# Key normalisation factors by a product with ones of the squared keys, instead of row sums turned into diagonal matrices

## The reference, cut to what matters

```
k = concatenate([k_nope, broadcast(k_pe)])      # 128 + 64 values a head
q = rms_norm_2(q, q_gain)
k = rms_norm_2(k, k_gain)                       # x * rsqrt(mean(x*x) + 1e-6) * gain
q = concatenate([q[..., :128], rope(q[..., 128:], pos)])
k = concatenate([k[..., :128], rope(k[..., 128:], pos)])
o = mla_attend(q, k, v, pos)                    # softmax of q k^T / sqrt(192), times v
x = x + (o * silu(gate)) @ w_out
```

## Time and profile before

| | before |
|---|---|
| three timed runs | 3512.02, 3507.12, 3512.03 us; median 3512.02 |
| the profiled execution | 3514.65 us |
| its span, first to last instruction | 3512.9 us |
| TensorE busy, share of the span | 96% |
| VectorE busy | 49% |
| ScalarE busy | 34% |
| mean granted clock of TensorE | 0.976 |

### The profile page before, as it was taken

One profiled execution on the slowest core, in us unless ns is written; L12 is line 12 of the kernel. 1 busy time (PEld: TensorE's weight loads), 2 busy tenths in 40 slices (PEclk: granted clock), 3 DMA queues, 4 the chain that ended last, 5 costly groups with the idle time before them and its releaser, 6 DMA issues. The chain is left out here.

```text
span 3512.9 us, 51809 instructions
## 1 busy us (share of the span) xinstructions
PE 3358.3 (96%) x21928; PEld 2646.9 (75%) x21928; DVE 1715.1 (49%) x2838; ACT 1190.1 (34%) x1864; POOL 112.0 (3%) x90
## 2 busy tenths in 40 slices
PE   4999999989999989989999999999999999999999
PEld 2877777767777778857786666787888778887687
DVE  3325555544555545364436556434454455544632
ACT  4113333423333322242224444332333333333421
POOL 1000000001001101100000000010000000000000
PEclk7999999999999989999999999999999999999999
DMA  5522333232212134232342112353322232322442
GB/s 172 139 68 78 93 91 96 81 88 72 63 51 80 52 107 146 83 120 75 95 122 69 36 46 77 96 157 96 96 84 85 75 91 87 91 87 75 150 136 87
DMA packets 492315, 324.38 MB, mean 92 GB/s; under 512 B 27050, under 2 KB 448397, under 8 KB 491446
## 3 DMA queue, kind: packets, MB, share of 16 engines
q1 hardware_dynamic: 492086, 321.08, 31.2%
HBM read 276.18 MB, written 44.85 MB: 91 GB/s over the span
## 5 line engine op out<-in xcount | busy, mean ns | idle before, releaser
L532 PE MATMUL PS<-XH,WHT 128*128 128x512 f32 x2256 | 929.4, 412 | 48.4 <-DVE WLT L520 33.4
L520 DVE TENSOR_TENSOR WLT<-AR,WHT 128x1024 fp32r<-128x1024 f32 (+1 forms) x430 | 520.7, 1214 | 858.0 <-ACT WHT L514 857.4
L534 PE MATMUL PS<-XH,WLT 128*128 128x512 f32 x2256 | 890.1, 395 | 0.0
L514 ACT ACTIVATE WHT<-AR 128x1024 fp32r<-128x1024 f32 (+1 forms) x430 | 446.6, 1041 | 751.8 <-PE PS L534 595.2
L533 PE MATMUL PS<-XL,WHT 128*128 128x512 f32 (+1 forms) x1744 | 684.6, 393 | 0.0
L532 PEld LDWEIGHTS PS<-XH,WHT 128*128 128x128 f32 x2256 | 426.1, 189 | 158.2 <-DVE WLT L520 34.3
L534 PEld LDWEIGHTS PS<-XH,WLT 128*128 128x128 f32 x2256 | 425.8, 189 | 99.7
L533 PE MATMUL PS<-ARR,WHT 128*128 128x512 f32 x1024 | 403.6, 394 | 0.0
L533 PEld LDWEIGHTS PS<-XL,WHT 128*128 128x128 f32 (+1 forms) x1744 | 328.8, 189 | 73.5 <-issue 4.8
L533 PEld LDWEIGHTS PS<-ARR,WHT 128*128 128x128 f32 x1024 | 193.9, 189 | 50.9 <-issue 8.6
L532 PE MATMUL PS<-XL,WHT 128*128 128x512 f32 x512 | 203.6, 398 | 0.0
(11 more groups left out here) (433 smaller groups left out, 5079.8 us busy)
## 6 DMA issues: line engine op xcount, KB each, us to landing
AR<-b_w_in SPq DMA_DIRECT2D x128, 512.0 KB, 4.0
AR<-w_in SPq DMA_DIRECT2D x122, 512.0 KB, 3.7
AR<-a_w_in SPq DMA_DIRECT2D x48, 512.0 KB, 4.3
AR<-w_out SPq DMA_DIRECT2D x32, 512.0 KB, 4.4
AR<-a_w_out SPq DMA_DIRECT2D x32, 512.0 KB, 4.0
AR<-b_w_out SPq DMA_DIRECT2D x32, 512.0 KB, 4.0
proj_scratch<-AR SPq DMA_DIRECT2D x33, 256.0 KB, 2.3
AR<-a_w_kv_up SPq DMA_DIRECT2D x32, 256.0 KB, 3.7
```

The lines of the kernel that those rows point to most:

```text
L514: self.nc.scalar.activation(self.shaped(self.high, n), self.shaped(self.raw, n), ACT.Copy).then_inc(self.s_high, 1)
L520: self.nc.vector.tensor_tensor(self.shaped(self.low, n), self.shaped(self.raw, n), f32(self.shaped(self.high, n)), ALU.subtract).then_inc( ...
L532: mm(out, wh, xh[k0 + c], start=(start and c == 0), stop=False)
L534: last = mm(out, wl, xh[k0 + c], start=False, stop=(stop and c == nk - 1))
```

## The change

- Key sums, their reciprocals and the diagonals are gone. `key_factors` multiplies ones by the squared keys themselves, so each of the 128 partitions of `FB[e]` holds every token's sum of squares. It stands at its old place, behind `value(i, 1)`; for pair 0 it takes the place of the key sums, behind tile 14.
- The mean is taken at full width, 128x512 a head, from `FB[e]` into `SQ` (`key_mean`), ScalarE takes its root (`key_root`), VectorE its reciprocal and then the two products (`keys`), all from `SQ`.
- `rotary` and `query` wait for the means, not for `kr0` and `kr1`. `query_square` waits for `kr0` and `kr1`, since it writes `SQ`.
- VectorE: the means stand behind `bias(i, 2)`; `keys(q, 0)` behind `scale(i, 2)`, `keys(q, 1)` behind `rotary_gain(q)`. ScalarE: the roots stand behind `value_copy(i, 1)`, not behind `split_high` of unit 4i + 4.
- The shared rotary part's share is kept 128x512 (`KPS`) and made by one product of full width. Constants that nothing uses leave the table: 264 of 2315 columns.

```
-            def key_sums(i):
-                N.wait(pe, i, "act.sk1")
-                N.wait(pe, i - 1, "dve.meanq")
-                if i == 0:
-                    pe.wait_ge(kp_c, 1)
-                sums(SQ[:, 0, :], 0)
-                N.did(sums(SQ[:, 1, :], TB), "pe", "kn")
             def key_factors(i, e):
-                N.wait(pe, i, f"dve.dg{e}")
+                N.wait(pe, i, f"act.sk{e}")
             def rotary(i):
-                N.wait(pe, i, "dve.kr0")
+                N.wait(pe, i, "dve.meank0")
-                    N.wait(pe, i, "dve.kr1")
+                    N.wait(pe, i, "dve.meank1")
             def rotary_sums(i):
                 N.wait(pe, i, "act.sqr")
+                N.wait(pe, i - 1, "dve.meanq")
             def rotary_key():
-                for tb in steps:
-                    last = mm(MB[:, tb:tb + 1], SQ[:, 2, blk(tb)], C("cmask", 0, 1), start=True, stop=True)
-                last.then_inc(kp_m, 1)
+                mm(MB[:, :], C("ones"), SQ[:, 2, :], start=True, stop=True).then_inc(kp_m, 1)
             def query_square(i, e):
-                N.wait(act, i, f"dve.cq{e}", f"pe.rk{e}")
+                N.wait(act, i, f"dve.cq{e}", f"dve.kr{e}")
+            def key_root(i, e):
+                N.wait(act, i, f"dve.meank{e}")
+                N.did(A(SQ[:, e, :], SQ[:, e, :], ACT.Sqrt), "act", f"rootk{e}")
                 st.split_high(act, UT + 4 * i + 4)
-                if more:
-                    root(q, "k")
                 exps(i, 2)
                 value_copy(i, 0)
                 copy(i, 1)
                 value_copy(i, 1)
+                if more:
+                    key_root(q, 0)
+                    key_root(q, 1)
                 st.split_high(act, UT + 4 * i + 5)
-            def key_diagonals(i): ...
+            def key_mean(i, e):
+                N.wait(dve, i, f"pe.rk{e}")
+                do(f"meank{e}", STT(out=SQ[:, e, :], in0=FB[e][:, :], scalar=1.0 / QK, in1=KPS, op0=ALU.mult, op1=ALU.add))
+            def keys(i, e):
+                N.wait(dve, i, f"act.rootk{e}")
+                r, x = SQ[:, e, :], KN[i % 2][:, e, :]
+                do(f"reck{e}", V.reciprocal(r, r))
+                N.wait(dve, i, f"dve.reck{e}")
+                do(f"kg{e}", STT(out=x, in0=x, scalar=GK, in1=r, op0=ALU.mult, op1=ALU.mult))
+                do(f"kr{e}", TTn(KR[rows(e), i % 2, :], KPR[rows(e), :], SQ[rows(e), e, :], ALU.mult))
                 scale(i, 1)
-                if more:
-                    key_means(q)
                 bias(i, 2)
                 if more:
-                    key_diagonals(q)
-                    keys(q)
+                    key_mean(q, 0)
+                    key_mean(q, 1)
                 st.split_low(dve, UT + 4 * i + 5)
                 scale(i, 2)
-                if not more:
+                if more:
+                    keys(q, 0)
+                else:
                     low(i - 1)
                 bias(i, 3)
                 if more:
                     rotary_gain(q)
+                    keys(q, 1)
                 output(i, 0)
```

More of the change, by code:

```diff
@@ L59 @@
 NPROJ = 62
-ARENA = 16800
-CONST = dict(ident=128, ones=128, bones=128, hone0=128, hone1=128, swap=128, flip=128, cen=128, eye=64, mt=256,
-             lev=(1 + len(LEVELS)) * 64, cmask=2, rst=512, freq=1, nslope=8)
+ARENA = 17064
+CONST = dict(ident=128, ones=128, bones=128, swap=128, flip=128, cen=128, eye=64, mt=256,
+             lev=(1 + len(LEVELS)) * 64, cmask=2, rst=512, freq=1)
 def const_cols():
@@ L2269, in latent @@
     RM, RS, RQ = take(24, 1), take(16, 1), [take(8, 1), take(8, 1)]
-    MX, GK, KPC = take(12, 1), take(1, 1), take(TB, 1)
+    MX, GK, KPS = take(12, 1), take(1, 1), take(T, 1)
     DM, COS, SIN = k.angles()
@@ L2291, in latent @@
     N = Marks(k, "mlap",
[L2292 to L2294 removed]
+              pe=["k0", "k1", "rk0", "rk1", "qr", "qn0", "sw", "qrs", "qn1", "qns"],
+              act=["sk0", "sk1", "rootk0", "rootk1", "sqr", "sq0", "sq1", "rootq"],
+              dve=["ck0", "ck1", "meank0", "meank1", "reck0", "kg0", "kr0", "qg", "reck1", "kg1", "kr1", "cq0", "sws", "qc", "qa", "cq1", "meanr", "meanq", "recq", "rq"])
     V_ = Marks(k, "mlav", pe=["a", "b"], act=["a", "b"])
@@ L2570, in _ @@
             after = {t: [lambda t=t: mean_square(t - 2)] for t in range(2, 10)}
-            after.update({10: [rotary_key], 11: [rotary_key_swap], 13: [lambda: key(0, 0), lambda: key(0, 1)], 14: [lambda: key_sums(0)],
-                          15: [lambda: key_factors(0, 0), lambda: key_factors(0, 1), lambda: rotary(0), lambda: query(0, 0)],
+            after.update({10: [rotary_key], 11: [rotary_key_swap], 13: [lambda: key(0, 0), lambda: key(0, 1)], 14: [lambda: key_factors(0, 0), lambda: key_factors(0, 1)],
+                          15: [lambda: rotary(0), lambda: query(0, 0)],
                           16: [lambda: swap(0), lambda: rotary_sums(0), lambda: query(0, 1)], 17: [lambda: query_sums(0)],
@@ L2645, in query_square, with query_root @@
             def query_square(i, e):
-                N.wait(act, i, f"dve.cq{e}", f"pe.rk{e}")
+                N.wait(act, i, f"dve.cq{e}", f"dve.kr{e}")
                 N.did(A(SQ[:, e, :], QN[i % 2][:, e, :], ACT.Square), "act", f"sq{e}")
[L2649 to L2652, removed]
+            def key_root(i, e):
+                N.wait(act, i, f"dve.meank{e}")
+                N.did(A(SQ[:, e, :], SQ[:, e, :], ACT.Sqrt), "act", f"rootk{e}")
+            def query_root(i):
+                N.wait(act, i, "dve.meanq")
+                N.did(A(RS[:, 2 * TB:4 * TB], RM[:, 2 * TB:4 * TB], ACT.Sqrt), "act", "rootq")
             def value_copy(i, j):
@@ L2782, in _ @@
                 if more:
-                    root(q, "q")
+                    query_root(q)
             high(NP - 1)
@@ L2822, in query_copy @@
                 do(f"cq{e}", V.tensor_copy(QN[i % 2][:, e, :], FB[1][:, :]))
[L2824 to L2842, removed]
+            def key_mean(i, e):
+                N.wait(dve, i, f"pe.rk{e}")
+                if i == 0:
+                    dve.wait_ge(kp_c, 1)
+                do(f"meank{e}", STT(out=SQ[:, e, :], in0=FB[e][:, :], scalar=1.0 / QK, in1=KPS, op0=ALU.mult, op1=ALU.add))
[6 more added lines that the diff above has]
+                do(f"kr{e}", TTn(KR[rows(e), i % 2, :], KPR[rows(e), :], SQ[rows(e), e, :], ALU.mult))
             def rotary_gain(i):
@@ L2985, in _ @@
             after = {6: [lambda: normed(0)], 7: [lambda: split_behind(0)], 10: [lambda: normed(1), rotary_key_gain], 11: [lambda: split_behind(1)], 12: [rotary_key],
-                     13: [lambda: key_copy(0, 0), lambda: key_copy(0, 1), lambda: st.split_low(dve, KU[0] + 3)], 14: [lambda: key_means(0), lambda: key_diagonals(0)],
-                     15: [lambda: keys(0), lambda: st.split_low(dve, QRU[0] + 3), lambda: rotary_gain(0), lambda: query_copy(0, 0), lambda: st.split_low(dve, QNU[0] + 3)],
+                     13: [lambda: key_copy(0, 0), lambda: key_copy(0, 1), lambda: st.split_low(dve, KU[0] + 3)], 14: [lambda: key_mean(0, 0), lambda: key_mean(0, 1)],
+                     15: [lambda: keys(0, 0), lambda: st.split_low(dve, QRU[0] + 3), lambda: rotary_gain(0), lambda: keys(0, 1), lambda: query_copy(0, 0), lambda: st.split_low(dve, QNU[0] + 3)],
                      16: [lambda: rotary_turn(0), lambda: query_copy(0, 1)], 17: [lambda: query_factors(0)]}
```

13 lines of the change are left out of this document (5 added, 8 removed).

## The result

The kernel after takes 3515.82 us (median of 16 runs, 3510.5 to 3525.43), the kernel before 3511.3 us beside it (16 runs, 3505.0 to 3520.01). The ratio is 1.0016, its 95% interval 1.0009 to 1.0023: about 5.6 us slower by the ratio (the two medians alone lie 4.5 apart), inside the 0.2% that I called no change, and still outside the noise of this many runs. I had forecast +10.3. The profiled execution of after took 3520.21 us, its span is 5.5 longer than the span of before (3512.9), and so the two traces can be laid side by side.

The account below looks back on a forecast made before the run. TensorE, busy 96% of the span, was taken as the bound, with VectorE's queue late next. -7.35 between input tiles and +18.0 over seven turns, less tenths for constants, gave +10.3 on 3512.0: 3522; own range 3516 to 3529, whole 3508 to 3534.

Parts of the forecast that it names:

- The stage between the input tiles: Behind tile 15: sums of 1.8, the 2.71 wait for `kr0` and 2.84 of slow clock go, together 7.35 us.
- VectorE's chain: From the split behind the roots VectorE never rests for 16.4 us; earlier split to query sums becomes 34.7 us, was 31.8.
- My rival in which they hide: Reciprocals fit VectorE's free 21 us a turn and products win: 3475, or 3493 if only one fits; chance 0.10.
- the clock will not be full: Second query product, behind a 3.55 us wait: low clock adds 2.2 us a turn, bounds 0 and 4.
- stays, a slow stretch there included: From query sums to the next transposes nothing changes; the slow stretch may go (-1.65 x 5) or come (+1.65 x 2).
- my first rival: Clock stays up at the query product, or its slow stretch replaces the one behind the query sums: 3510, chance 0.25.
- The first stretch of a turn: From transposes to `value(i, 0)`: without key sums and their slow clock 4.3 us won a turn, about 30 in seven.
- The table load: Ahead of ScalarE's first root: 1.28 us, no drain; rival with a pause of about 1.35 gives 3531, chance 0.03.

Follow-up runs that it names:

- The filled wait: Kernel after with 26 products of 256 columns into an unused part of a bank ahead of `query(q, 1)`, so TensorE is not idle: 3523.8 us, ratio 1.0035.
- the short reciprocals: Kernel after with both key reciprocals on 8 of 512 columns, leaving the other columns' factors wrong: 3474.94 us, ratio 0.9901.
- the version on ScalarE: Kernel after with the key factor as exp(-0.5 ln(mean)) on ScalarE and no reciprocal on VectorE: 3489.56 us, ratio 0.9942.

## Why the prediction came out as it did

**The stage between the input tiles** was right: -7.35 said, -7.1 measured. The wait for `kr0` and the slow clock behind it went.

**VectorE's chain** was right. From split to end of copy I said 16.4, and it measured 16.6. From the earlier split to the query sums I said 34.7, and it measured 34.3 (1965.05 to 1999.31, turn 2), 34.2 to 35.1 over the seven turns. The waits were said to be 3.55 at the copy and 0.95 at `swap`, and measured 3.44 and 0.84. Shortening the reciprocals removed both waits and 41 us, so it is their time that made the change slower. My rival in which they hide gave 3475 for both and 3493 for one; with their time taken away the kernel ran in 3474.94 and 3489.89.

**The step that was mis-sized** is the clock. I wrote that "the clock will not be full", with 2.2 us more on the second query product, and that what follows the query sums "stays, a slow stretch there included". The first was 1.8 on the mean (the product took 5.05, 5.29 and then 4.43 to 4.52, where I had 5.05): about 2.6 us less over seven turns. The second was wrong. Before, the scores behind the query sums were slow (4.45 to 4.60 instead of 2.95) in five of seven turns; after, only in the first two. Three slow stretches of 1.65 left, 5.0 us. These counts are of one execution each. Against them stand 0.2 us a turn more of VectorE and a rest of the program 2 us longer than said, which is the slow stretch behind the rotary key and not the change. Together that is about the difference between +10.3 and +5.5, so errors of both signs stand in it, and part of the nearness is luck. Of the slow stretches the seven behind the key sums went, seven at the query product came, and three of the five behind the query sums went; my first rival held that the new ones take the place of the latter, and for three of them they did. The filled wait shows it from the other side: with the query product at full clock the slow stretch was back behind the sums. The answer lies between forecast and first rival: 3515.8 is just under the forecast's own range (3516 to 3529), inside the whole one (3508 to 3534), and within the 0.2% of no change to which I had given 0.33.

Two slips in the sums change nothing: -7.35 + 18.0 is +10.65, and in the first rival turn 6 should have +0.6 and not +1.1, as its distance before was 32.3.

**The first stretch of a turn** (4.3 us won a turn by products instead of sums) was right in size. In turn 1 it is 7.9 us from the first transposes to `value(i, 0)` before (1908.06 to 1916.00) and 3.7 after (1904.47 to 1908.21), 4.2 less; and the short reciprocals ran 35 us under before, where I had summed 37.

**The table load.** The root starts 0.01 us after the load's end (1973.04 + 1.28, 1974.33), and the same holds for both loads of the version on ScalarE (1912.23 + 1.28, 1913.52; 1914.86 + 1.28, 1916.16). The drain of about 1.38 us a switch that the Trainium skill (ScalarE: Activation LUTs, "What ACT_TABLE_LOAD costs") adds is not seen in any of them, and the chain of 34.3 has no room for it.

## What to carry to other kernels

An engine that is busy for half of the span was the late one here: ask what stands in its queue ahead of the step that the full engine waits for, and price the slowest instruction there (3.34 us for a reciprocal of 128x512, against 0.7 for a product of that size). The same change without reciprocals on VectorE won 20 us, and 36 with one more move. Before a thin product is replaced by a full one, try to move it: put it behind full products that cover the wait for its input; here two such moves gave 26 us where the replacement lost 5.6. And where a wait can't be removed, let full products follow it and not thin ones: much the same wait (24.1 and 26.4 us over seven turns) cost 21 us more when transposes and sums stood behind it.

## What the runs showed of the hardware that I had not expected

- A slow stretch of TensorE can take the place of another. With 3.44 us of idle time at the query product, the sums 6 us later brought one on in two turns of seven, where it had been five; with that idle time filled, it was there in all seven. The same in the kernel before: with the slow stretch behind the key sums gone, the one behind the query sums came in seven turns and not in five.
- Thin products next to a short idle time are enough to lower the clock: 0.6 us (2.3 in turn 0) and sums of 1.81 cost about 1.65 us on the scores behind, in 12 of 14 places of the kernel before. The same sums without the idle time, behind full products, cost almost none of it (44.4 us at the low clock in the loop, then 6.8).
- The length of a wait alone does not set what it costs behind it. Behind the same wait of 3.44 the query product took 4.43 to 5.29 in after, and 5.01 to 5.11 with the query sums moved; I have no run that tells what decides.
